# Final stage of a hybrid decoder step: the last two products of the sample rows and of token tile 1 go to ScalarE and GpSimd

## The reference

```python
    xp = xp + f[:n_prompt_tokens].reshape(xp.shape)
    xs = xs + f[n_prompt_tokens:].reshape(xs.shape)
    ...
y_prompt = rms_norm(xp, norm_final_w)
y_sample = rms_norm(xs, norm_final_w)

def rms_norm(x, g):
    y = x * lax.rsqrt(jnp.mean(x * x, axis=-1, keepdims=True) + RMS_EPS)
    return y * g
```

## Time and profile before

| what | value |
|---|---|
| median of three runs | 1113.7 us |
| the profiled execution's own time | 1114.5 us |
| its span, first to last instruction | 1112.8 us |
| mean granted TensorE clock | 0.973 |
| busy, share of the span: PE, PEld | 91%, 69% |
| busy: DVE, ACT, POOL | 51%, 33%, 40% |

### The profile page before, as it was taken

One profiled execution on the slowest core, in us unless ns is written; L12 is line 12 of the kernel. 1 busy time (PEld: TensorE's weight loads), 2 busy tenths in 40 slices (PEclk: granted clock), 3 DMA queues, 4 the chain that ended last, 5 costly groups with the idle time before them and its releaser, 6 DMA issues. The chain is left out here.

```text
span 1112.8 us, 24781 instructions
## 1 busy us (share of the span) xinstructions
PE 1014.0 (91%) x10429; PEld 766.1 (69%) x10429; DVE 564.1 (51%) x1195; ACT 364.7 (33%) x783; POOL 442.7 (40%) x458
## 2 busy tenths in 40 slices
PE   5999999789989999999999999999976999988883
PEld 4777777578878887888888888884554555554441
DVE  5587678656555643777645446324362322211126
ACT  3444544545545443444344451000111111111111
POOL 7646546244654424877663335410001222221110
PEclk9999999899999999999999999999986999999897
DMA  8122121110000007541242214407976999999965
GB/s 257 32 79 70 58 81 38 42 43 4 4 4 4 4 4 185 166 113 39 56 145 91 76 53 174 151 2 273 372 294 253 416 414 416 415 417 416 416 276 227
DMA packets 84935, 183.11 MB, mean 165 GB/s; under 512 B 9921, under 2 KB 59613, under 8 KB 76122
## 3 DMA queue, kind: packets, MB, share of 16 engines
q1 hardware_dynamic: 78173, 168.59, 41.6%
q0 software_dynamic: 5168, 8.56, 2.1%
q10 hardware_dynamic: 1485, 4.39, 1.0%
HBM read 173.24 MB, written 17.55 MB: 171 GB/s over the span
## 5 line engine op out<-in xcount | busy, mean ns | idle before, releaser
L2298 POOL DMA_INDIRECT d_y<-tl_xn,ex_sidx x32 | 31.9, 996 | 121.1 <-DVE tl_xn L2810 110.9
L2806 DVE SCALAR_TENSOR_TENSOR ex_sg<-tl_psA,ex_slot_rs,ex_sg 128x128 f32<-128x128 f32 x32 | 11.2, 351 | 134.2 <-ACT ex_sg L2606 134.1
L2293 POOL DMA_INDIRECT tl_xn<-d_tok,ex_gidx x17 | 17.8, 1048 | 143.7 <-DVEq L2798 78.1
L264 PE MATMUL psv<-xT,w_sum 128*128 128x260 f32 x256 | 61.6, 384 | 1.1 <-DVE uv_gu L1597 0.6
L226 POOL TENSOR_TENSOR w_sum<-w 128x512 f32<-128x512 f32 x16 | 21.2, 1324 | 94.1 <-PE mg_w L264 93.8
L264 PEld LDWEIGHTS psv<-xT,w_sum 128*128 128x128 f32 x256 | 48.4, 190 | 9.6 <-issue 1.0
L2606 ACT ACTIVATE ex_sg<-tl_psA,ex_slot_rs 128x128 f32<-128x128 f32 x32 | 11.7, 367 | 126.8 <-PE tl_psA L2464 126.8
L1060 PE MATMUL ck_b<-ck_X,ck_V 64*64 64x64 f32 x1280 | 50.4, 222 | 3.2 <-issue 2.1
L264 PE MATMUL rk_ps<-xT,rk_w 128*128 128x260 f32 x208 | 50.1, 384 | 0.0
L264 PE MATMUL rk_ps<-xS,rk_w 128*128 128x260 f32 x200 | 48.6, 386 | 0.0
L1060 PEld LDWEIGHTS ck_b<-ck_X,ck_V 64*64 64x64 f32 x1280 | 43.0, 134 | 4.4 <-issue 4.1
(11 more groups left out here) (617 smaller groups left out, 2789.4 us busy)
## 6 DMA issues: line engine op xcount, KB each, us to landing
wd<-in_moe_w_down SPq DMA_DIRECT2D x13, 1024.0 KB, 23.7
rk_w<-in_w_in SPq DMA_DIRECT2D x12, 1024.0 KB, 5.4
w_uv<-in_w_in SPq DMA_DIRECT2D x16, 512.0 KB, 5.2
w<-in_w_in SPq DMA_DIRECT2D x8, 1024.0 KB, 5.8
tl_x<-in_moe_w_down SPq DMA_DIRECT2D x8, 1024.0 KB, 21.7
xT<-in_moe_w_gate SPq DMA_DIRECT2D x5, 1024.0 KB, 16.9
xT<-in_moe_w_up SPq DMA_DIRECT2D x5, 1024.0 KB, 19.5
bonus_all<-in_moe_w_gate SPq DMA_DIRECT2D x5, 1024.0 KB, 19.5
```

Of the source, the lines that this page charges most:

```text
L264: ins = eng.matmul(bank[:, 0:TH], w[:, k, :], x[:, k, :], start=(first and k == 0), stop=(last and k == NK // 2 - 1), skip_group_check=True)
L2293: eng.indirect_dma_start(out=xg[:, p % 2, :], out_offset=None, in_=m.d_tok, in_offset=bass.IndirectOffsetOnAxis(ap=gidx[:, p:p + 1], axis= ...
L2298: eng.indirect_dma_start(out=m.d_y2, out_offset=bass.IndirectOffsetOnAxis(ap=rows, axis=0), in_=yo[:, x, :], in_offset=None, bounds_check= ...
L2806: eng.scalar_tensor_tensor(out=sg[:, out, :], in0=psg[out][:, P:2 * P], scalar=scale, in1=sg[:, out, :], op0=ALU.mult, op1=ALU.mult).then_ ...
```

## The change

The products of the sample rows and of tile 1 leave VectorE's list. ScalarE multiplies these rows by their root (an activation `Copy` with a scale for each partition, in place), GpSimd multiplies the result by the gain (a `tensor_tensor`, in place). VectorE tells ScalarE with `s_root` that a root is there, by a `sem_inc` instruction of its own after `root(0, 1)` and after `root(1, 3)`; ScalarE tells GpSimd with `s_rows`; GpSimd tells SyncE with `s_gain`. In ScalarE's list both copies stand between the square of tile 1 and the square of tile 2. The order in which SyncE writes the groups out stays.

```diff
@@ the semaphores
-        s_fx, s_diag, s_fp, s_fs, s_fsq, s_fo, s_out = \
-            (sem("f_" + n) for n in ("x", "diag", "p", "s", "sq", "o", "out"))
+        s_fx, s_diag, s_fp, s_fs, s_fsq, s_fo, s_root, s_rows, s_gain, s_out = \
+            (sem("f_" + n) for n in ("x", "diag", "p", "s", "sq", "o", "root", "rows", "gain", "out"))
@@ sync
-            for i, j in enumerate(final):
-                eng.wait_ge(s_fo, i + 1)
+            for j, s_from, count in ((NT, s_gain, 1), (0, s_fo, 1), (1, s_gain, 2), (2, s_fo, 2), (3, s_fo, 3)):
+                eng.wait_ge(s_from, count)
@@ gpsimd, at its end
+            eng.wait_ge(s_fx, 16 * (NT + 2))
+            eng.wait_ge(s_rows, 1)
+            eng.tensor_tensor(fxs, fxs, gf[0:TS, :], ALU.mult).then_inc(s_gain, 1)
+            eng.wait_ge(s_rows, 2)
+            eng.tensor_tensor(fx[:, 1, :], fx[:, 1, :], gf[:, :], ALU.mult).then_inc(s_gain, 1)
@@ scalar
             square_final(2, fx[:, 1, :], P)
+            eng.wait_ge(s_root, 1)
+            eng.activation(fxs, fxs, ACT.Copy, scale=rstd[0:TS, 0:1]).then_inc(s_rows, 1)
+            eng.wait_ge(s_root, 2)
+            eng.activation(fx[:, 1, :], fx[:, 1, :], ACT.Copy, scale=rstd[:, 2:3]).then_inc(s_rows, 1)
             eng.wait_ge(s_fp, 2)
@@ vector
             sum_up(NT)
             root(0, 1)
+            eng.sem_inc(s_root, 1)
             sum_up(1)
-            scaled(0, fxs, fxs, gf[0:TS, :])
             root(1, 3)
+            eng.sem_inc(s_root, 1)
             sum_up(3)
             scaled(1, psA[:, :, :], by_half(fx[:, 0, :]), by_half(gf[:, :]))
-            scaled(2, fx[:, 1, :], fx[:, 1, :], gf[:, :])
             root(3, 5)
             scaled(3, psT[:, :, :], by_half(fx[:, 2, :]), by_half(gf[:, :]))
             scaled(4, fx[:, 3, :], fx[:, 3, :], gf[:, :])
```

## The result

The changed kernel takes 1116.99 us (median of 20 runs, 1111.91 to 1123.39), the kernel before 1113.13 us in 20 runs beside it (1109.43 to 1117.46). The ratio is 1.0029, 95% interval 1.0015 to 1.0043, which is 3.2 us (1.7 to 4.8); the two medians are 3.9 us apart. It is 0.3% slower, as forecast.

A forecast was written before the change was run, and what follows sets the result against it. VectorE, working nearly without a gap behind the last expert, was taken as the bound. 2.17 + 0.12 + 2.11 - 1.08 = +3.3 us on the median 1113.7 gives 1117.0 us, range 1114.5 to 1118.6.

The forecast's parts named there:

- first hold: In `root(1, 3)`, an L92 waits for GpSimd's product of the sample rows: +2.17 us, bounds 0 to 2.65.
- second `sem_inc`: Behind `root(1, 3)` on VectorE, ahead of `sum_up(3)`: the added instruction costs the path 0.12 us.
- second hold: Second half of `sum_up(3)` waits on VectorE for GpSimd's product of tile 1: +2.11 us, bounds 0.0 to 2.6.
- `scaled(2)` not ahead of `root(3, 5)`: With the product of tile 1 off VectorE, `root(3, 5)` could start directly behind ScalarE's sum: gain 1.08 us.
- GpSimd's time on 8 rows: GpSimd's product of the sample rows takes 2.35 us, going by columns for each partition; bounds 0.3 to 2.83 us.
- Rival B: GpSimd's product on 8 rows is short, first hold 0.1 to 0.3 us, second stays: +1.2, 1114.9 us; chance 0.10.
- When GpSimd starts on the sample rows: GpSimd starts at 1098.1, 0.08 us behind ScalarE's copy of the sample rows, which ends at 1098.0.
- That VectorE is held: VectorE instructions with two SBUF inputs and GpSimd instructions reading SBUF exclude each other; read from L177, 8 columns, 2.35 us.
- rival C: At both hold places the products pass each other, so only `sem_inc` and gain remain: -1.0, 1112.7 us; chance 0.12.
- Who goes next: At `sum_up(3)`, GpSimd asks during the first half and, standing waiting, has SBUF next, from 1102.69 to 1105.04.
- Rival A: Second half of `sum_up(3)` goes before GpSimd, which then holds an L90 of `root(3, 5)`: +1.8, 1115.5 us; chance 0.13.
- Rival D: Both GpSimd products take 2.83 us, 0.5 us more for each hold: +4.3, 1118.0 us; chance 0.07.

The follow-up runs named there:

- run without the products: Changed kernel with GpSimd's two products left out; F (start of TensorE's combination of tile 0 to end of VectorE's last product) 18.41 us, ratio 0.9993.
- the one with memsets: Changed kernel with each GpSimd product replaced by two memsets of 1024 columns into scratch rows, so GpSimd only writes; F 18.40 us, against 22.54 in the changed kernel.
- the run with the later request: Changed kernel with one more ScalarE copy of 256 columns ahead of the copy of tile 1; F 21.45 us, ratio 1.0013 to the kernel before.
- the run with tile 1 alone: Changed kernel with the product of the sample rows back on VectorE; F 20.48 us, ratio 1.0029 to the kernel before.

## Why the prediction was right

The forecast was 1117.0 us, measured were 1116.99, with a range and a direction that held. That the median agrees to the last digit is luck: the interval of the ratio alone is 3 us wide, and the kernel before came out at 1113.13 beside it, not at the 1113.7 on which the forecast stands. What counts is that the terms agree one by one:

| term | predicted | profile after |
|---|---|---|
| first hold, an L92 in `root(1, 3)` | +2.17 | 2.34 - 0.16 = +2.18 |
| second `sem_inc` | +0.12 | 1097.51 - 1097.35 = 0.16, before 0.04: +0.12 |
| second hold, second half of `sum_up(3)` | +2.11 | 4.57 - 2.61 = +1.96 |
| `scaled(2)` not ahead of `root(3, 5)` | -1.08 | 1103.30 - 1102.08 = 1.22, before 2.30: -1.08 |
| sum | +3.3 | +3.18 |

- *The size of the gain at stake* came from the view in order of time: the product that leaves costs 1.28 us, but only 1.08 of it stood before something that was ready.
- *GpSimd's time on 8 rows* was taken from rows of 128 partitions, 2.35 us; it was 2.33. Rival B, that it goes by rows, is out. Its price was summed too low: +1.2 leaves out the 0.1 to 0.3 us of first hold that it allows, so it is 1.3 to 1.5.
- *When GpSimd starts on the sample rows* came out right by two small errors that cancel: ScalarE's copy started 0.1 us earlier than I had it (1092.90, 7.48 us after the start of F, not 7.58), and GpSimd started 0.19 us behind its end (1094.03), not 0.08.
- *That VectorE is held* rested on one early stretch. The run without the products and the one with memsets show that it is GpSimd's reading and nothing else of the change; both holds were there, so rival C is out.
- *Who goes next* was the step with the least margin. GpSimd asked at 1098.67, 0.12 us before the end of the first half (1097.51 + 1.28 = 1098.79) and 0.17 before the second half started (1098.84), and took its turn; its 2.34 us show no wait. I had let it begin at the end of the first half, and this accounts for 0.12 of the 0.15 us by which the second hold is shorter than predicted. So the forecast's reason, that the one that stands waiting goes next, was not what decided here: GpSimd came first and did not have to wait. None of the runs made GpSimd wait while VectorE had another instruction with two SBUF inputs ready to go, so that reason rests on the earlier trace rows alone. Rival A happens when GpSimd asks 0.4 us later, as its run showed, and costs 2.1 us instead of 1.8.
- *Rival D*, 2.83 us for a GpSimd product, did not come: both took 2.33 to 2.34. That length in the earlier trace rows had a wait for VectorE in it, as the 3.27 us in the run with the later request had.
- *The last store* was to be issued near 1112.0. It was at 1107.99, which is 1111.90 once the 3.91 us of the earlier start are added.

## What to carry to other kernels

Before work is moved from VectorE to GpSimd, look at what VectorE runs at that time: beside a GpSimd instruction that reads SBUF, a VectorE instruction with two inputs in SBUF waits, on two columns (2.18 us here) as long as on 1024 (1.96 to 2.07), and both engines show the wait as busy time. A product with an input in PSUM did not wait. A chain of short dependent instructions is a bad neighbour, since whatever holds one of them holds the path. In this kernel, what VectorE needn't do late was better done by VectorE early, in a wait that the profile shows: 0.96 us of the stage. It has to be checked first that the data has landed there.

## What the runs showed of the hardware that I had not expected

A VectorE instruction with one input in SBUF can be held too. In the run with the later request the `TENSOR_SCALAR` on L2947, 128x2 float32 in SBUF, started at 1102.37 and took 1.02 us, where it takes 0.17 alone; it ended at 1103.39, 0.03 after GpSimd's product (1103.36). I had counted it as free. The Trainium skill, page "SBUF — State Buffer", section "Who interferes with whom", counts `tensor_scalar` among those that can take both ways of VectorE into SBUF, when their operands meet its conditions, and this row agrees. In the same run the product with an input in PSUM was not held (1.28 us).

By an estimate from these rows, VectorE lets go of SBUF some 0.12 us before the end that the profile shows: GpSimd's product that asked at 1100.09 and lasts 2.34 us alone must have begun at 1101.02, and the instruction that it waited for is shown until 1101.15 (1098.54 + 2.61). It fits that GpSimd's product of tile 1 showed no wait although it started 0.12 us before the end of the first half in the changed kernel, and 0.02 us before it (1095.84 against 1094.58 + 1.28 = 1095.86) in the run with tile 1 alone.
